# Seven-block products from output pair 4 in the four later feed-forward stages, their token sums made later and closer together

## The chip, the cores and the metric

One core of a Trainium2 chip runs the whole program. The metric is the device time of one execution in microseconds. The core has TensorE (matrix products into PSUM banks), VectorE, ScalarE and GpSimd, each with its own in-order stream of instructions, and SyncE, which issues most of the weight transfers. The engines meet only at semaphores.

## The reference, cut to what matters

512 tokens of width 1024 pass through two blocks of two layers each. The program holds six feed-forward products of one form (inner width 2816):

```python
def swiglu(h, w_in, w_out):
    g, u = jnp.split(h @ w_in, 2, axis=-1)
    return (jax.nn.silu(g) * u) @ w_out
```

The first four stand in a block with adaptive norms (a gain and a shift from a conditioning vector), the last two in one with plain RMS norms (`silu(g_part) * u_part`, the same product). Between them lie a pooling mixer, an attention, and two mixers of four branches. All is float32.

## The kernel before, in words

**Precision.** Each operand of a product is split into a high part (rounded to the fast float32 form, `F32R`) and a low part (the rest). A product of two is three matmuls: high by high, high by low, low by high. ScalarE makes high parts with a copy, VectorE low parts with a subtraction.

**Weights.** SyncE loads units of 128 columns by 1024 rows (512 KB) into four slots of `stage`. For each unit ScalarE makes `w_hi` (line 866, in `convert`), then VectorE `w_lo` (line 1600, its `convert`). Two pairs of `w_hi`/`w_lo` take turns, and a third pair (`third_hi`, `third_lo`) serves special units. A slot is loaded again once both parts of its unit are made.

**A feed-forward stage.** The 2816 inner columns are FC = 22 chunks of 128. An *output pair* is one chunk of gate and one of up, so there are 22 pairs, two to a *step* of four units: gate and up of the even pair, gate and up of the odd. In the text a *column* of a step is its c, 0 to 3. Plain form (`products`, lines 2604 to 2606): a unit is 8 chunks of the inner dimension times three matmuls of 512 tokens, 24 matmuls. ScalarE takes silu of the gate bank (`sg`), VectorE multiplies with the up bank, and the result is split for the output product, which follows the 22 pairs (`step_out`).

**The seven-block form.** In stages with `i >= SEVEN_FFN` (the third to the sixth) the later pairs are made otherwise. Gate and up columns, the two halves of the 1024 inner rows and the two halves of the tokens make a product of 2 by 2 by 2 blocks, done with seven block products instead of eight. A block (`block`, lines 2733 to 2735) is 4 chunks times three matmuls of 256 tokens, 12 matmuls. It needs sums of the weight blocks (`part_sums`, `second_sum`, `fourth_sum` on VectorE, then `sum_high` on ScalarE and `sum_low` on VectorE, anew for each pair) and four sums of the normed tokens, made once for a stage: `t_sum(0..3)` on VectorE, the high parts `t_high(0..3)` on ScalarE (line 955), the low parts `t_low(0..3)` on VectorE (line 1837). Sum 1 builds on sum 0, sum 3 on sum 1. In the third and fourth stages sums 1 to 3 are four operations each (line 1831), because a shift enters, in the fifth and sixth each is one (line 1825).

**Order in the opening.** `SEVEN_FROM` plain steps come first (`opening_step`), 3 before: pairs 0 to 5. In them VectorE and ScalarE have, beside their ordinary work, the token sums in an order written out by hand: `T_WORK` says after which (step, column) VectorE does which sum or low part, `T_HIGHS` after which ScalarE does which high part. In the last opening step, column 2, the weight sums of the first seven-block pair are made; `sum_high(0)` and `sum_low(0)` come ahead of `convert(c + 2)`, which prepares the row weights that the first block reads. Column 3 has the second weight sum, whose high part waits until TensorE has done all opening units. Then `seven_step` runs for the other steps, the first and last unrolled, the middle ones in a loop.

In the first block TensorE waits for `w_lo` of the row weights:

```python
pe.wait_ge(silu_ready, n.pair + 5)
pe.wait_ge(w_lo_ready, n.unit + 13)
block(GATE[0][:, 0:H], weights(n.unit + 12, 0), 1, of_h(4, 0), True).then_inc(product_done, 1)
```

**Late splits.** The products of seven-block pairs, and of the last opening step, are kept whole (`wk(k)`) and split late: `late_high(k)` on ScalarE (line 974) and `late_low(k)` on VectorE (line 1869), in the last pair and ahead of the output product. Products of earlier steps are split at once (lines 997 and 1905).

Of the kernel before, what the change touches and what calls it, by code (L numbers as in the profile page):

```python
# [37 lines left out]
WORDS = 8 * P  # L38
# [7 lines left out]
H = S // 2  # L46
SEVEN_FROM = 3
SEVEN_PAIRS = FC - 2 * SEVEN_FROM

# [49 lines left out]
def build(nc, A, out):  # L99
    ctx = ExitStack()  # L100
    with ctx:
# [95 lines left out]
        w_lo_ready = sem("w_lo_ready")  # L197
# [653 lines left out]
        def _(act):  # L851
# [80 lines left out]
            def ffn(i):  # L932
# [24 lines left out]
                def sum_high(which, at_, done):  # L957

                    dst = third_hi[:] if which == 0 else weights(n.unit + 13, 0)[0]
                    act.wait_ge(sums_ready, done)  # L960
                    nc.scalar.activation(dst, sums[:, which * 2 * S:(which + 1) * 2 * S], ACT.Copy) \
                        .then_inc(sum_hi_ready, 1)

                def late_high(k):

                    pb = 6 * SEVEN_PAIRS * (n.seven + 1)
                    act.wait_ge(prod_ready, n.pair + k + 1)
                    if k < 6:
                        act.wait_ge(unit_done, n.unit + 2 * FC - 2)
                    elif k < 18:  # L970
                        act.wait_ge(product_done, pb - (3 if k < 10 else 2 if k < 14 else 0))
                    else:
                        act.wait_ge(unit_done, n.unit + 2 * FC)
                    nc.scalar.activation(chunk(a_lo, k), wk(k), ACT.Copy).then_inc(a_hi_ready, 1)

                def opening_step(j):

                    for c in range(4):
                        p = n.pair + 2 * j + c // 2
                        raw = n.norm - 1 in RAW and j == 0  # L980
                        if j == 2 and c == 2:
                            sum_high(0, 0, 3 * SEVEN_PAIRS * n.seven + 3)
                        if j == 2 and c == 3:
                            act.wait_ge(unit_done, n.unit + 12)
                            sum_high(1, 0, 3 * SEVEN_PAIRS * n.seven + 2)
                        elif not raw or c == 3:
                            convert(c + 2, j)
                        if c % 2 == 0 and raw:
                            act.wait_ge(raw_scaled, RAW.index(n.norm - 1) // 2 * 2 + c // 2 + 1)
                            nc.scalar.activation(chunk(sg, p % 2), chunk(sg, p % 2), ACT.Silu).then_inc(silu_ready, 1)  # L990
                        elif c % 2 == 0:
                            act.wait_ge(unit_done, n.unit + 4 * j + c + 1)
                            act.wait_ge(prod_ready, p - 1)
                            nc.scalar.activation(chunk(sg, p % 2), GATE[p % 2][:], ACT.Silu).then_inc(silu_ready, 1)
                        elif j < 2:
                            act.wait_ge(prod_ready, p + 1)
                            nc.scalar.activation(chunk(a_lo, 2 * j + c // 2), chunk(prod, p % 2), ACT.Copy) \
                                .then_inc(a_hi_ready, 1)
                        if (j, c) in T_HIGHS:
                            t_high(T_HIGHS.index((j, c)))  # L1000

                def seven_step(step):
# [9 lines left out]
                    for r in range(2):  # L1012
# [6 lines left out]
                        if not first:  # L1019
# [9 lines left out]
                        act.wait_ge(w_loaded[slot], 16 * ((u0 + 2 * r + 2) // STAGES + 1) + 16 * step)  # L1029
                        nc.scalar.activation(weights(u0 + 12, 0)[0], stage[:, slot * WORDS:(slot + 1) * WORDS],  # L1030
                                             ACT.Copy).then_inc(w_hi_ready, 1)
# [4 lines left out]
                        if end:  # L1036
                            late_high(4)

                        act.wait_ge(product_done, count(6, 4))
                        nc.scalar.activation(snap_second, up[:, 0:H], ACT.Copy).then_inc(snap_ready, 1)  # L1040
                        if end:
                            for k in (5, 6, 7):
                                late_high(k)
                        else:
                            sum_high(1, r, count(3, 5))
# [16 lines left out]
                if i >= SEVEN_FFN:  # L1062
                    for j in range(SEVEN_FROM):
                        opening_step(j)
                    seven_steps(act, seven_step)
                    slot = (n.unit + 45) % STAGES
                    act.wait_ge(w_loaded[slot], 16 * ((n.unit + 45) // STAGES + 1))
                    nc.scalar.activation(weights(n.unit + 45, 0)[0], stage[:, slot * WORDS:(slot + 1) * WORDS],
                                         ACT.Copy).then_inc(w_hi_ready, 1)
                    fourth_snap(1, n.unit + 2 * FC, n.pair + FC - 1)  # L1070
                    for k in range(8, 16):
                        late_high(k)
                else:
                    looped(act, FC // 2, step_in)
# [508 lines left out]
        def _(dve):  # L1583
# [193 lines left out]
            def ffn(i, s):  # L1777
# [83 lines left out]
                def sum_low(which, done):  # L1861
                    hi, lo = (third_hi[:], third_lo[:]) if which == 0 else weights(n.unit + 13, 0)
                    dve.wait_ge(sum_hi_ready, done)
                    nc.vector.tensor_tensor(lo, sums[:, which * 2 * S:(which + 1) * 2 * S], hi.bitcast(F32),
                                            ALU.subtract).then_inc(sum_lo_ready, 1)
# [5 lines left out]
                def opening_step(j):  # L1871
                    f, u0 = n.seven, n.unit
                    for c in range(4):
                        p = n.pair + 2 * j + c // 2
                        u = u0 + 4 * j + c
                        raw = n.norm - 1 in RAW and j == 0
                        if j == 2 and c == 2:
                            dve.wait_ge(a_ready, n.pair + 4)
                            part_sums(u0 + 12, 0)
                            second_sum(u0 + 12, 0, 3 * SEVEN_PAIRS * f + 1)  # L1880
                            fourth_sum(u0 + 12, 0, 3 * SEVEN_PAIRS * f + 2)
                            sum_low(0, 2 * SEVEN_PAIRS * f + 1)
                        if j == 2 and c == 3:
                            t_low(3)
                            sum_low(1, 2 * SEVEN_PAIRS * f + 2)
                        elif not raw or c == 3:
                            convert(c + 2, j)
# [7 lines left out]
                        elif c % 2:  # L1895
                            dve.wait_ge(silu_ready, p + 1)
                            dve.wait_ge(unit_done, u + 1)
                            if j == 1:
                                dve.wait_ge(a_ready, p - 1)
                            dst = chunk(prod, p % 2) if j < 2 else wk(2 * j + c // 2)  # L1900
                            nc.vector.tensor_tensor(dst, chunk(sg, p % 2), UP[p % 2][:], ALU.mult).then_inc(prod_ready, 1)
                        if c % 2 and j < 2:
                            k = 2 * j + c // 2
# [15 lines left out]
                def seven_step(step):  # L1919
# [5 lines left out]
                    for r in range(2):  # L1925
# [12 lines left out]
                        if not end:  # L1938
                            second_sum(u, step, count(3, 4))
                            fourth_sum(u, step, count(3, 5))  # L1940
                        hi, lo = weights(u0 + 12, 0)
                        slot = u % STAGES
# [3 lines left out]
                        if end:  # L1946
                            late_low(4)

# [3 lines left out]
                        if end:  # L1952
                            for k in (5, 6, 7):
                                late_low(k)
# [6 lines left out]
                if i >= SEVEN_FFN:  # L1961
                    for j in range(SEVEN_FROM):
# [5 lines left out]
                    nc.vector.tensor_tensor(lo, stage[:, slot * WORDS:(slot + 1) * WORDS], hi.bitcast(F32),  # L1968
                                            ALU.subtract).then_inc(w_lo_ready, 1)
                    late_low(8)  # L1970
                    pairs = SEVEN_PAIRS * (n.seven + 1)
# [621 lines left out]
        def _(pe):  # L2593
# [92 lines left out]
            def ffn(i):  # L2686
# [64 lines left out]
                def seven_step(step):  # L2751
                    first, last = (isinstance(step, int) and step == s_ for s_ in (SEVEN_FROM, FC // 2 - 1))
                    f, u0, p0 = n.seven, n.unit, n.pair
                    rows = weights(u0 + 12, 0)
                    s21, s34 = weights(u0 + 13, 0), (third_hi, third_lo)

# [6 lines left out]
                    for r in range(2):  # L2763
# [24 lines left out]
                        if not (last and r == 1):  # L2788
                            if first and r == 0:
                                pe.wait_ge(silu_ready, p0 + 6)  # L2790
                            else:
# [9 lines left out]
                if i >= SEVEN_FFN:  # L2801
                    for j in range(SEVEN_FROM):
                        opening_step(j)
                    pe.wait_ge(silu_ready, n.pair + 5)
                    pe.wait_ge(w_lo_ready, n.unit + 13)
                    block(GATE[0][:, 0:H], weights(n.unit + 12, 0), 1, of_h(4, 0), True).then_inc(product_done, 1)
                    seven_steps(pe, seven_step)
# [713 lines left out]
for at_, step_ in enumerate(STAGE_ORDER):  # L3521
    if step_[0] in ("fox", "mix") or step_[0] == "ffn" and step_[1] >= 2:
# [5 lines left out]
KEPT = (3, 5, 7, 9)  # L3528
T_HIGHS = [(0, 3), (1, 1), (1, 3), (2, 0)]
T_WORK = {(0, 1): (("sum", 0),), (0, 3): (("sum", 1),), (1, 0): (("low", 0),), (1, 1): (("sum", 2),),  # L3530
          (1, 2): (("low", 1),), (1, 3): (("sum", 3),), (2, 0): (("low", 2),)}
TOTAL_UNITS = sum(UNITS_OF[s[0]] for s in STAGE_ORDER)
# [93 lines left out]
```

## Time and profile before

| | |
|---|---|
| median of 3 runs | 3654.19 us (3652.86 to 3658.12) |
| the profiled execution | 3653.87 us |
| its span, first to last instruction | 3652.1 us |
| TensorE busy | 3573.9 us (98%), 18986 matmuls |
| VectorE busy | 2157.6 us (59%) |
| ScalarE busy | 1604.8 us (44%) |
| mean granted TensorE clock | 0.993 |
| DMA | 388.72 MB, mean 106 GB/s |

The span is counted from the first instruction; 1.8 us of the execution lie around it. A granted clock of 1 is 2.4 GHz, 0.5 is 1.2 GHz. Durations of matmuls overlap with the next ones, so their rate is read from how many fit in a stretch and not from the duration of one. In the trace the four stages begin their seven-block products at 898.30, 1540.60, 2451.46 and 3362.25 us.

### The profile page before, as it was taken

The page shows a single profiled execution, that of the slowest core. Times are in us where ns is not written, and L with a number is a line of the kernel's source. Part 1 is how long each engine was busy: PE and PEld are TensorE (multiplying, and loading weights), DVE is VectorE, ACT ScalarE, POOL GpSimd, SP SyncE. Part 2 cuts the span into 40 slices and gives each one's busy share as a digit, 9 for nine tenths or more (in the row PEclk, how much of TensorE's full clock was granted, in tenths as well). Part 3 has the DMA queues.
Part 4 walks back from the last instruction along what each step waited for, and adds up shares of the span by engine and source line. Part 5 has one row for each costly group of instructions (what it writes and reads, how often), then busy time and mean ns, then how long its engine had stood idle before and what let it go on. Part 6 is the DMA issues. An engine that isn't in the chain of part 4 may idle for free.

```text
span 3652.1 us, 52186 instructions
## 1 busy us (share of the span) xinstructions
PE 3573.9 (98%) x18986; PEld 2922.6 (80%) x18986; DVE 2157.6 (59%) x3118; ACT 1604.8 (44%) x2666; POOL 87.2 (2%) x74
## 2 busy tenths in 40 slices
PE   7999999999999999999999999999999999999999
PEld 5888778888998777899867677889986767788997
DVE  6843488426873654687355556478735565647862
ACT  3232432224553554455354444355535454435552
POOL 0000100000000000000000000000000000000000
PEclk9999999999999999999999999999999999999999
DMA  9843278433333222333322222333332222233332
GB/s 313 275 127 95 85 251 278 140 99 91 104 104 94 58 58 58 93 104 100 95 80 65 62 70 61 91 93 104 101 103 72 69 58 74 57 91 93 104 104 87
DMA packets 643164, 388.72 MB, mean 106 GB/s; under 512 B 17969, under 2 KB 602545, under 8 KB 642993
## 3 DMA queue, kind: packets, MB, share of 16 engines
q1 hardware_dynamic: 640256, 381.41, 35.8%
q10 hardware_dynamic: 2736, 4.98, 0.4%
q8 instruction: 113, 1.85, 0.2%
q14 instruction: 59, 0.48, 0.0%
HBM read 384.23 MB, written 2.10 MB: 106 GB/s over the span
## 4 chain that ended last, share of the span: by engine, by line
PE 90%; DVE 5%; ACT 2%; issue 1%; SPq 1%; DMA 0%; POOL 0%; DVEq 0%; ACTq 0%; POOLq 0%
PE bank L2604 20%; PE bank L2605 20%; PE bank L2606 20%; PE bank L2733 6%; PE bank L2735 6%; PE bank L2734 6%; PE bank L2910 1%; PE bank L2975 1%; PE bank L2891 1%; PE bank L3126 1%; PE bank L2893 1%; PE bank L2892 1%; DVE w_lo L1600 1%; DVE work L2279 1%; PE bank L3192 1%
## 5 line engine op out<-in xcount | busy, mean ns | idle before, releaser
L1600 DVE TENSOR_TENSOR w_lo<-stage,w_hi 128x1024 fp32r<-128x1024 f32 x432 | 528.8, 1224 | 834.8 <-ACT w_hi L866 834.5
L2604 PE MATMUL bank<-h_hi,w_hi 128*128 128x512 f32 x2088 | 844.0, 404 | 13.3 <-ACT gs L1145 4.8
L2606 PE MATMUL bank<-h_hi,w_lo 128*128 128x512 f32 x2088 | 818.7, 392 | 0.0
L2605 PE MATMUL bank<-h_lo,w_hi 128*128 128x512 f32 x2088 | 818.6, 392 | 0.0
L866 ACT ACTIVATE w_hi<-stage 128x1024 fp32r<-128x1024 f32 x432 | 456.9, 1058 | 750.7 <-PE bank L2606 741.9
L2604 PEld LDWEIGHTS bank<-h_hi,w_hi 128*128 128x128 f32 x2088 | 395.1, 189 | 127.9 <-issue 30.0
L2605 PEld LDWEIGHTS bank<-h_lo,w_hi 128*128 128x128 f32 x2088 | 395.6, 189 | 84.1 <-issue 6.7
L2606 PEld LDWEIGHTS bank<-h_hi,w_lo 128*128 128x128 f32 x2088 | 395.0, 189 | 84.5
L2604 PE MATMUL bank<-a_lo,w_hi 128*128 128x512 f32 x704 | 274.6, 390 | 0.0
L2606 PE MATMUL bank<-a_lo,w_lo 128*128 128x512 f32 x704 | 274.0, 389 | 0.0
L2605 PE MATMUL bank<-a_hi,w_hi 128*128 128x512 f32 x704 | 274.0, 389 | 0.0
L2606 PEld LDWEIGHTS bank<-a_lo,w_lo 128*128 128x128 f32 x704 | 132.2, 188 | 27.7
L2605 PEld LDWEIGHTS bank<-a_hi,w_hi 128*128 128x128 f32 x704 | 132.2, 188 | 27.1
L2604 PEld LDWEIGHTS bank<-a_lo,w_hi 128*128 128x128 f32 x704 | 132.2, 188 | 26.9
L2735 PE MATMUL bank<-h_hi,w_lo 128*128 128x256 f32 x512 | 144.9, 283 | 0.0
L2733 PE MATMUL bank<-work_r,w_hi 128*128 128x256 f32 x512 | 144.9, 283 | 0.0
L2734 PE MATMUL bank<-work_r,w_hi 128*128 128x256 f32 x512 | 144.9, 283 | 0.0
L2735 PE MATMUL bank<-work_r,w_lo 128*128 128x256 f32 x512 | 144.9, 283 | 0.0
L2734 PE MATMUL bank<-h_lo,w_hi 128*128 128x256 f32 x512 | 144.9, 283 | 0.0
L2733 PE MATMUL bank<-h_hi,w_hi 128*128 128x256 f32 x512 | 144.9, 283 | 0.0
L2606 PE MATMUL bank<-a_hi,w_lo 128*128 128x512 f32 x352 | 136.9, 389 | 0.0
L2604 PE MATMUL bank<-a_hi,w_hi 128*128 128x512 f32 x352 | 136.9, 389 | 0.0
(421 smaller groups left out, 6734.9 us busy)
## 6 DMA issues: line engine op xcount, KB each, us to landing
stage<-in_ffn_w_in SPq DMA_DIRECT2D x176, 512.0 KB, 3.9
stage<-in_w_in SPq DMA_DIRECT2D x108, 512.0 KB, 3.8
stage<-in_w_gate_up SPq DMA_DIRECT2D x88, 512.0 KB, 3.8
ada_stage<-in_ada_w SPq DMA_DIRECT2D x128, 256.0 KB, 4.4
work<-in_ada_w SPq DMA_DIRECT2D x128, 256.0 KB, 6.5
stage<-in_ffn_w_out SPq DMA_DIRECT2D x64, 512.0 KB, 3.9
stage<-in_w_down SPq DMA_DIRECT2D x32, 512.0 KB, 4.2
stage<-in_ffn_w_out SPq DMA_DIRECT2D x32, 384.0 KB, 3.4
```

Of the source, the lines that this page charges most:

```text
L866: nc.scalar.activation(weights(u, per * i)[0], stage[:, slot * WORDS:(slot + 1) * WORDS], ACT.Copy).then_inc(w_hi_ready, 1)
L1600: nc.vector.tensor_tensor(lo, stage[:, slot * WORDS:(slot + 1) * WORDS], hi.bitcast(F32), ALU.subtract).then_inc(w_lo_ready, 1)
L2279: nc.vector.tensor_tensor(part, part, other, ALU.mult).then_inc(hfac_ready, 1)
L2604: nc.tensor.matmul(dst, wh, chunk(hi, k), start=first and a == 0, stop=False)
L2605: nc.tensor.matmul(dst, wh, chunk(lo, k), start=False, stop=False)
L2606: ins = nc.tensor.matmul(dst, wl, chunk(hi, k), start=False, stop=last and a == len(ks) - 1)
L2733: nc.tensor.matmul(dst, wh, xh, start=first and k == 0, stop=False, skip_group_check=True)
L2734: nc.tensor.matmul(dst, wh, xl, start=False, stop=False, skip_group_check=True)
L2735: ins = nc.tensor.matmul(dst, wl, xh, start=False, stop=k == 3, skip_group_check=True)
L2891: nc.tensor.matmul(bank[7][:], wh, hi, start=c == 0, stop=False)
L2892: nc.tensor.matmul(bank[7][:], wh, lo, start=False, stop=False)
L2893: ins = nc.tensor.matmul(bank[7][:], wl, hi, start=False, stop=c == 1)
```

## The change

`SEVEN_FROM` goes from 3 to 2. Pairs 4 and 5 of the third to the sixth stage are made in seven blocks too (18 pairs instead of 16 in each), and two opening steps are left. What was tied to the last opening step moves to step 1: the weight sums, `sum_high` and `sum_low`, and the uses of `weights(...)` with a number in them are written by `SEVEN_FROM`. The products of pairs 2 and 3 are now split late. `late_high` and `late_low` of chunks 2 and 3 take the place in the last pair that chunk 4 had, chunks 4 to 6 that of 5 to 7, and chunk 7 joins the later ones. `T_WORK` and `T_HIGHS` are rewritten: the sums begin one column later in step 0 and end in step 1, column 1; the high parts 0 and 1 come together in step 0, column 3; low part 3 comes after the product of step 1, column 3, where it was ahead of it and of the second weight sum's low part.

```diff
-SEVEN_FROM = 3
+SEVEN_FROM = 2
 ...
-                    dst = third_hi[:] if which == 0 else weights(n.unit + 13, 0)[0]
+                    dst = third_hi[:] if which == 0 else weights(n.unit + 4 * SEVEN_FROM + 1, 0)[0]
 ...
-                    if k < 6:
+                    if k < 4:
+                        pass
+                    elif k < 6:
                         act.wait_ge(unit_done, n.unit + 2 * FC - 2)
 ...
-                        if j == 2 and c == 2:
+                        if j == SEVEN_FROM - 1 and c == 2:
                             sum_high(0, 0, 3 * SEVEN_PAIRS * n.seven + 3)
-                        if j == 2 and c == 3:
-                            act.wait_ge(unit_done, n.unit + 12)
+                        if j == SEVEN_FROM - 1 and c == 3:
+                            act.wait_ge(unit_done, n.unit + 4 * SEVEN_FROM)
                             sum_high(1, 0, 3 * SEVEN_PAIRS * n.seven + 2)
 ...
-                        elif j < 2:
+                        elif j < SEVEN_FROM - 1:
 ...
-                        if (j, c) in T_HIGHS:
-                            t_high(T_HIGHS.index((j, c)))
+                        for which in T_HIGHS.get((j, c), ()):
+                            t_high(which)
 ...
                         if end:
-                            late_high(4)
+                            for k in (2, 3):
+                                late_high(k)
 ...
-                            for k in (5, 6, 7):
+                            for k in (4, 5, 6):
                                 late_high(k)
 ...
-                    for k in range(8, 16):
+                    for k in range(7, 16):
                         late_high(k)
 ...
-                        if j == 2 and c == 2:
-                            dve.wait_ge(a_ready, n.pair + 4)
-                            part_sums(u0 + 12, 0)
-                            second_sum(u0 + 12, 0, 3 * SEVEN_PAIRS * f + 1)
-                            fourth_sum(u0 + 12, 0, 3 * SEVEN_PAIRS * f + 2)
+                        if j == SEVEN_FROM - 1 and c == 2:
+                            dve.wait_ge(a_ready, n.pair + 2 * SEVEN_FROM - 2)
+                            part_sums(u0 + 4 * SEVEN_FROM, 0)
+                            second_sum(u0 + 4 * SEVEN_FROM, 0, 3 * SEVEN_PAIRS * f + 1)
+                            fourth_sum(u0 + 4 * SEVEN_FROM, 0, 3 * SEVEN_PAIRS * f + 2)
                             sum_low(0, 2 * SEVEN_PAIRS * f + 1)
-                        if j == 2 and c == 3:
-                            t_low(3)
+                        if j == SEVEN_FROM - 1 and c == 3:
                             sum_low(1, 2 * SEVEN_PAIRS * f + 2)
 ...
+                    late_low(7)
                     late_low(8)
 ...
-                    pe.wait_ge(silu_ready, n.pair + 5)
-                    pe.wait_ge(w_lo_ready, n.unit + 13)
-                    block(GATE[0][:, 0:H], weights(n.unit + 12, 0), 1, of_h(4, 0), True).then_inc(product_done, 1)
+                    pe.wait_ge(silu_ready, n.pair + 2 * SEVEN_FROM - 1)
+                    pe.wait_ge(w_lo_ready, n.unit + 4 * SEVEN_FROM + 1)
+                    block(GATE[0][:, 0:H], weights(n.unit + 4 * SEVEN_FROM, 0), 1, of_h(4, 0), True).then_inc(product_done, 1)
 ...
-T_HIGHS = [(0, 3), (1, 1), (1, 3), (2, 0)]
-T_WORK = {(0, 1): (("sum", 0),), (0, 3): (("sum", 1),), (1, 0): (("low", 0),), (1, 1): (("sum", 2),),
-          (1, 2): (("low", 1),), (1, 3): (("sum", 3),), (2, 0): (("low", 2),)}
+T_HIGHS = {(0, 3): (0, 1), (1, 0): (2,), (1, 1): (3,)}
+T_WORK = {(0, 2): (("sum", 0),), (0, 3): (("sum", 1),), (1, 0): (("low", 0), ("sum", 2)),
+          (1, 1): (("sum", 3), ("low", 1)), (1, 2): (("low", 2),), (1, 3): (("low", 3),)}
```

## Rows read from the trace of the kernel before

**Rows 1.** The page: busy time (share) xinstructions, and the chain by engine.
```profile
PE 3573.9 (98%) x18986; PEld 2922.6 (80%) x18986; DVE 2157.6 (59%) x3118; ACT 1604.8 (44%) x2666; POOL 87.2 (2%) x74
...
PE 90%; DVE 5%; ACT 2%; issue 1%; SPq 1%; DMA 0%; POOL 0%; DVEq 0%; ACTq 0%; POOLq 0%
```

**Rows 2.** Waits of TensorE, 838 to 1062 us: total, times, longest.
```profile
PE bank L2733 <- ACT rstd L1049: 0.5, 1, 0.5
```

**Rows 3.** Windows by engine (us, busy (x), clock, DMA); timeline of TensorE.
```profile
843.90:898.30 54.40, 54.40 (x242) 45.05 (x240) 32.32 (x42) 20.31 (x25) 0.00 (x0) 1.00 0.34 98
898.30:1058.14 159.84, 159.84 (x1333) 159.78 (x1331) 131.54 (x173) 92.81 (x160) 0.00 (x0) 1.00 0.37 107
...
2451.46 0.28 PE L2733 MATMUL bank<-h_hi,w_hi 128*128 128x256 f32 x1
```

**Rows 4.** Timeline of VectorE, third stage: start, us, line, out<-in [idle before].
```profile
859.26 1.67 DVE L1831 SCALAR_TENSOR_TENSOR work<-work,mod 128x256 f32<-128x256 f32 x4
...
870.14 0.16 DVE L1828 TENSOR_TENSOR shift_step<-mod 128x4 f32<-128x4 f32 x1
870.34 1.68 DVE L1831 SCALAR_TENSOR_TENSOR work<-work,shift_step 128x256 f32<-128x256 f32 x4
...
889.91 0.68 DVE L1901 TENSOR_TENSOR work<-sg,bank 128x512 f32<-128x512 f32 x1
890.51 0.69 DVE L1848 TENSOR_TENSOR sums<-stage 128x512 f32<-128x512 f32 x1
...
894.38 1.23 DVE L1864 TENSOR_TENSOR third_lo<-sums,third_hi 128x1024 fp32r<-128x1024 f32 x1 [1.13 <-ACT third_hi L961]
895.52 1.22 DVE L1600 TENSOR_TENSOR w_lo<-stage,w_hi 128x1024 fp32r<-128x1024 f32 x1
...
901.33 0.69 DVE L1848 TENSOR_TENSOR sums<-stage 128x512 f32<-128x512 f32 x1
...
904.47 1.22 DVE L1944 TENSOR_TENSOR w_lo<-stage,w_hi 128x1024 fp32r<-128x1024 f32 x1
```

**Rows 5.** Timeline of ScalarE, third stage.
```profile
858.52 1.05 ACT L955 ACTIVATE work_r<-work 128x1024 fp32r<-128x1024 f32 x1
860.48 1.06 ACT L866 ACTIVATE w_hi<-stage 128x1024 fp32r<-128x1024 f32 x1 [0.91 <-PE bank L2606]
...
893.28 1.06 ACT L961 ACTIVATE third_hi<-sums 128x1024 fp32r<-128x1024 f32 x1 [4.54 <-DVE sums L1858]
894.25 1.04 ACT L866 ACTIVATE w_hi<-stage 128x1024 fp32r<-128x1024 f32 x1
...
898.50 1.06 ACT L961 ACTIVATE w_hi<-sums 128x1024 fp32r<-128x1024 f32 x1 [2.72 <-PE bank L2606]
```

**Rows 6.** Timeline of VectorE, fifth stage.
```profile
2414.56 1.22 DVE L1825 TENSOR_TENSOR work<-work 128x1024 f32<-128x1024 f32 x1
```

**Rows 7.** Timeline of ScalarE, fifth stage.
```profile
2414.77 1.04 ACT L866 ACTIVATE w_hi<-stage 128x1024 fp32r<-128x1024 f32 x1
```

**Rows 8.** Timeline of ScalarE at the end of the third stage's seven-block pairs.
```profile
1060.77 4.27 ACT L974 ACTIVATE a_lo<-work 128x512 fp32r<-128x512 f32 x8
1066.02 1.06 ACT L866 ACTIVATE w_hi<-stage 128x1024 fp32r<-128x1024 f32 x1 [0.98 <-PE bank L2606]
```

**Rows 9.** Windows, TensorE alone: us, busy (x), granted clock, DMA share, GB/s.
```profile
412.42:414.56 2.14, 0.00 (x2) 1.00 0.54 214
414.72:418.13 3.41, 3.41 (x17) 0.50 0.00 0
...
448.86:455.69 6.83, 5.86 (x11) 0.50 0.00 0
468.35:470.22 1.87, 0.00 (x1) 1.00 0.89 302
470.22:475.00 4.78, 4.78 (x21) 1.00 0.64 189
...
1206.62:1210.03 3.41, 3.41 (x9) 0.50 0.52 144
```

More of the change, by code:

```diff
@@ L1029, in seven_step @@
                         act.wait_ge(w_loaded[slot], 16 * ((u0 + 2 * r + 2) // STAGES + 1) + 16 * step)
-                        nc.scalar.activation(weights(u0 + 12, 0)[0], stage[:, slot * WORDS:(slot + 1) * WORDS],
+                        nc.scalar.activation(weights(u0 + 4 * SEVEN_FROM, 0)[0], stage[:, slot * WORDS:(slot + 1) * WORDS],
                                              ACT.Copy).then_inc(w_hi_ready, 1)
@@ L1861, in sum_low @@
                 def sum_low(which, done):
-                    hi, lo = (third_hi[:], third_lo[:]) if which == 0 else weights(n.unit + 13, 0)
+                    hi, lo = (third_hi[:], third_lo[:]) if which == 0 else weights(n.unit + 4 * SEVEN_FROM + 1, 0)
                     dve.wait_ge(sum_hi_ready, done)
@@ L1897, in opening_step @@
                             dve.wait_ge(unit_done, u + 1)
-                            if j == 1:
+                            if 0 < j < SEVEN_FROM - 1:
                                 dve.wait_ge(a_ready, p - 1)
-                            dst = chunk(prod, p % 2) if j < 2 else wk(2 * j + c // 2)
+                            dst = chunk(prod, p % 2) if j < SEVEN_FROM - 1 else wk(2 * j + c // 2)
                             nc.vector.tensor_tensor(dst, chunk(sg, p % 2), UP[p % 2][:], ALU.mult).then_inc(prod_ready, 1)
-                        if c % 2 and j < 2:
+                        if c % 2 and j < SEVEN_FROM - 1:
                             k = 2 * j + c // 2
@@ L1940, in seven_step @@
                             fourth_sum(u, step, count(3, 5))
-                        hi, lo = weights(u0 + 12, 0)
+                        hi, lo = weights(u0 + 4 * SEVEN_FROM, 0)
                         slot = u % STAGES
@@ L1946, in seven_step @@
                         if end:
-                            late_low(4)
+                            for k in (2, 3):
+                                late_low(k)
                         dve.wait_ge(product_done, count(6, 5))
@@ L1952, in seven_step @@
                         if end:
-                            for k in (5, 6, 7):
+                            for k in (4, 5, 6):
                                 late_low(k)
@@ L2753, in seven_step @@
                     f, u0, p0 = n.seven, n.unit, n.pair
-                    rows = weights(u0 + 12, 0)
-                    s21, s34 = weights(u0 + 13, 0), (third_hi, third_lo)
+                    rows = weights(u0 + 4 * SEVEN_FROM, 0)
+                    s21, s34 = weights(u0 + 4 * SEVEN_FROM + 1, 0), (third_hi, third_lo)
                     def count(per, plus):
@@ L2789, in seven_step @@
                             if first and r == 0:
-                                pe.wait_ge(silu_ready, p0 + 6)
+                                pe.wait_ge(silu_ready, p0 + 2 * SEVEN_FROM)
                             else:
```

## The prediction

> **What bounds the kernel now.** I read the page first: TensorE is busy 98% of the span and holds 90% of the chain that ended last [rows 1]. The span is TensorE's time, so an edit pays only by taking TensorE cycles away and costs only by letting it wait. Next, the waits of the third feed-forward stage from its first product to its last: in 220 us TensorE waits once, 0.5 us [rows 2]. The same view of the fifth stage says the same.
>
> Then the cost of a product. One output pair (128 gate and 128 up columns) takes 48 matmuls of 512 columns in the plain form, 84 of 256 columns in the seven-block form. The durations (390 and 280 ns) overlap, so I take the rate from the windows. The plain stretch 843.90 to 898.30 holds 240 matmuls (242 shown, two begun before it): 54.40/240 = 226.7 ns. The seven-block stretch 898.30 to 1058.14 holds 111 blocks of 12: 159.84/1332 = 120.0 ns [rows 3]. So a pair costs 48 x 0.2267 = 10.88 us plain, 84 x 0.120 = 10.08 us in seven blocks, and a unit (24 plain matmuls) 5.44 us.
>
> **What the change takes away.** Two more pairs (4 and 5) of each of four stages: 8 x 0.80 = 6.4 us less. The 0.5 us wait of the last pair stays. That is 0.18% of the run. About 0.2% (7.3 us) is what a measurement of this kernel can tell from no change.
>
> The Trainium skill (TensorE: Matmul & The Clock Gate, section "Back-to-back issue gap") gives about columns/2.4 + 2.5 ns, which is 216 and 109 ns here; by that the estimate for a pair is 10.36 against 9.17 us, and for the eight pairs 9.5 us. The measured 120 ns of the 256-column form decides against it.
>
> **What the change moves.** Before, three opening steps (12 units, 65 us) covered the preparation of four token sums: four sums and four low parts on VectorE, four high parts on ScalarE. Now all but the last low part has to happen ahead of block products that begin after two steps. The work itself is not larger, but it is a chain across two in-order engines. I follow it in the third stage with the durations and hand-over times of the rows: an operation of 1024 columns starts its successor on VectorE after 1.14 us, on ScalarE after 0.97; the other engine sees its end 0.03 us later. The seven-block part was to begin at 898.30 and would now be due at 898.30 - 4 x 5.44 = 876.54.
>
> - Step 0, column 3: sum 1 (four operations, L1831) runs 859.26 to 860.93 [rows 4]. ScalarE, after high part 0 (858.52, [rows 5]), now waits for it: high part 1 at 860.96. The conversion w_hi of unit 6, queued behind it, moves from 860.48 to 861.93, end 862.98. TensorE needs unit 6 at 865.66: hidden.
> - Step 1, column 0 on VectorE: w_lo of unit 6 863.01, low 0 864.15, sum 2 865.29; from its small operation to its end 1.88 us (870.14 to 872.02, [rows 4]), so 867.17. ScalarE: high part 2 at 867.20, and behind it w_hi of unit 7 at 868.17, end 869.22.
> - Column 1: w_lo of unit 7 869.25 to 870.48; TensorE needs it at 871.10: 0.6 us spare. Product 870.39, sum 3 871.00 to 872.67, low 1 872.61; the next can start at 873.75.
> - Column 2: the four weight sums take from 890.51 until 893.28, when ScalarE takes up `third_hi` [rows 4, 5], 2.77 us; so `third_hi` at 876.52, and w_hi of unit 8 behind it at 877.49, end 878.53. VectorE: `third_lo` 877.61, w_lo of unit 8 878.75 to 879.97.
>
> Unit 8 is the row weights of the first block product. Before, its w_lo was made from 895.52 to 896.74, 1.56 us ahead of need [rows 4]. Now TensorE, due at 876.54, waits until 880.00: a stall of **3.46 us**. The fourth stage runs the same operations with the same shapes, so I give it the same stall.
>
> In the fifth and sixth stages the sums are single operations of 1.22 us, but they start later against the products: sum 1 ends at 2415.78, 3.0 us before unit 6 is due (4.7 us in the third stage) [rows 6]. High part 1 2415.81; w_hi of unit 6 2416.78 instead of 2414.77 [rows 7]; its w_lo ends at 2419.08, and unit 6 is due at 2418.82 (the first block, 2451.46 [rows 3], less six units): 0.3 us of waiting. Low 0 2419.00, sum 2 2420.14, high 2 2421.39, w_hi of unit 7 2422.36, its w_lo ends 2424.67 against 2424.56: 0.14 more. Product 2424.58, sum 3 2425.19, low 1 2426.33, weight sums 2427.47, `third_hi` 2430.24, w_hi of unit 8 2431.21, `third_lo` 2431.33, w_lo of unit 8 ends 2433.70. The block product, due at 2429.70 + 0.44, waits 3.58 us. Together **4.02 us**.
>
> What is late next? Low 2 and the second weight sum follow on VectorE and end at 882.23; the third block needs it at 880.00 + 2.88 = 882.88. ScalarE's high part of it (once tied to the end of the last plain unit, 898.50, [rows 5]) now comes before the first block. Low 3, moved behind the product, delays the next weight sums by 1.1 us: they start 3.87 us after the first block instead of 3.03 (901.33, [rows 4]), and the row weights of the next pair end 8.2 us after it. Before it was 7.4 (904.47 + 1.22), and the sixth block needs them at 8.64: no stall, 0.4 us spare. Were that gone, each 0.1 us late would cost 0.1 us a stage.
>
> **The tail.** Chunks 2 and 3 of the products are now converted late: two more ScalarE operations of 0.53 us and two VectorE operations of 0.6. One of each goes into idle time of the last pair, one falls behind the last pair, where eight late operations take 4.27 us on ScalarE and ScalarE is then idle 0.98 us before the next w_hi [rows 8]. That idle covers 0.53; I cost it at nothing, and at 4 x 0.5 = 2 us if the cover is gone. They replace operations inside the opening, which are no longer on the path. Weight loads keep their trigger (w_lo) and the stage buffer is four units deep; unit 9, which the weight sums need, is asked for once w_lo of unit 5 is made, which is before sum 1 (859.26), over 14 us ahead of 873.75: nothing.
>
> Stalls: 2 x 3.46 + 2 x 4.02 = 15.0. Less 6.4 gained: **+8.6 us**.
>
> **TensorE's clock.** Each stall leaves the array idle some 3.3 us. After the 2.14 us of idle before 414.56 the granted clock fell to 0.50 for 3.41 us (1.2 instead of 2.4 GHz); after 1.87 us it stayed at 1.00 [rows 9]. Five idle stretches are longer than 2.1 us, that one the shortest, and half rate followed all five. In such a stretch, from 1206.62, 9 matmuls of 512 columns were under way, one of them begun before; at full rate it would be 15. At half rate a 256-column matmul takes an estimated 213 ns (half of what 512 columns take there, 3.41/8), so 3.41 us holds 16 instead of 28: 1.5 us lost, less where the slow stretch begins in the idle time. I take 1.15 per stall, 4.6 in all; the bounds are 0 and 4 x 3.0 (two such stretches each, as at 448.86, 6.83 us [rows 9]).
>
> Sum: 8.6 + 4.6 = 13.2. The profiled execution has 3653.87 us (span 3652.1 and 1.8 around it), the median of the three is 3654.19. So 3653.87 + 13.2 = 3667.1, and on the median **3667.4 us**, +0.36%.
>
> **Rivals.**
> 1. Stalls, no slow clock: 3654.2 + 8.6 = 3662.8, +0.24%. For it: 1.87 us of idle did nothing. Against it: five of five longer ones did.
> 2. The stall is half as long: what ScalarE's waits for the sums put ahead of the conversions (w_hi of unit 6 alone is 1.45 us late, 861.93 against 860.48) passes beside other work. 15.0/2 - 6.4 = +1.1, and the clock perhaps +1: 3655 to 3657, the same.
> 3. The other side: w_lo of unit 8 is ready when due. VectorE is busy 32.3 of the 54.4 us before the first block [rows 3], so throughput is there; this decides if the chain of column 2 begins 3.5 us earlier than 873.75. Then only the 6.4 us remain: 3647.8, -0.18%, the same by the bound. Against it: sum 3 sits behind the product of column 1, and what follows adds up to 6.2 us from fixed durations.
> 4. A 256-column matmul in steady state costs half of a 512-column one, 113.3 ns, and nothing stalls: 84 x 0.1133 = 9.52 us, 1.36 us a pair, 8 x 1.36 = 10.9: 3643.3, faster by 0.30%. The windows measure 120.0 ns over 1332 matmuls, so next to no chance. The Trainium skill, in the section named above, puts it at 109 ns.
> 5. More is late: the 0.4 us of spare at the sixth block goes, and two slow stretches follow each stall. 3667.4 + 4 x 1.85 + 4 x 0.5 = 3677.
>
> **Numbers.** Forecast 0.48, rival 1 0.25, rival 2 0.11, rival 3 0.06, rival 4 0.01, rival 5 0.09. Slower (above 3661.5): 0.48 + 0.25 + 0.09, less 0.04 for a rival 1 that ends just under the bound, 0.78. Same: 0.11 + 0.06 + 0.04 = 0.21. Faster: 0.01. The range 3657 to 3673 leaves out rivals 3, 4 and 5 and the lower part of rival 2, some 0.2. The forecast's own range is 3663 to 3672.
>
> **What would show it.** In the changed kernel: one TensorE wait of about 3.5 us in each of stages 3 to 6, at the first 256-column product, put down to VectorE's w_lo (the conversion at L1600 here); two small ones before units 6 and 7 in stages 5 and 6 alone; granted clock 0.50 for 3.4 us behind most of them; in each stage 168 more matmuls of 256 columns and 96 fewer of 512; no new wait in the tail. Wrong would be: no wait at the first block (chain shorter than its rows say), waits at the third or sixth block, or a seven-block pair that does not take 10.08 us.

## The result and the profile after

| | before | after |
|---|---|---|
| median of 5 runs | 3654.43 us (3652.86 to 3658.12) | 3671.84 us (3667.81 to 3673.62) |
| ratio, 95% interval | | 1.0043 (1.0032 to 1.0053) |
| the profiled execution's span | 3652.1 us | 3670.6 us |
| matmuls | 18986 | 19274 |

The medians differ by 17.4 us, 0.48%: the change makes the kernel slower. The ratio is estimated at 1.0043, and its interval is 12 to 19 us. The forecast was +13.2 us (3667.4), with a range from 3657 to 3673; the median lies 4.4 us above the forecast and 1.2 us inside the end of the range.

The page of the changed kernel, busy time (share) xinstructions, then the chain that ended last by engine; these answer to [rows 1]:

```profile
PE 3578.9 (98%) x19274; PEld 2938.8 (80%) x19274; DVE 2197.6 (60%) x3182; ACT 1628.7 (44%) x2722; POOL 87.1 (2%) x74
...
PE 86%; DVE 7%; ACT 3%; issue 2%; SPq 1%; DMA 0%; POOL 0%; DVEq 0%; ACTq 0%; POOLq 0%
```

TensorE's share of the chain fell from 90 to 86%, VectorE's rose from 5 to 7%: the end now hangs on VectorE at some places. TensorE's waits over the whole span say where (total, times, longest), and its waits in the third stage, 838 to 1068 us, answer to [rows 2]:

```profile
PE bank L2737 <- DVE w_lo L1603: 13.3, 4, 3.3
...
PE bank L2737 <- DVE w_lo L1603: 3.3, 1, 3.3
PE bank L2737 <- ACT rstd L1052: 0.5, 1, 0.5
...
PE bank L2608 <- DVE w_lo L1603: 0.3, 1, 0.3
```

The last line is of the fifth stage, the wait before unit 6. Line 2737 is the block product's first matmul, line 1603 the `w_lo` conversion: four waits, one a stage. None of these was there before. In the timeline of TensorE the wait is the idle time ahead of the first 256-column matmul:

```profile
878.91 0.39 PE L2610 MATMUL bank<-h_hi,w_lo 128*128 128x512 f32 x1
882.64 0.55 PE L2737 MATMUL bank<-h_hi,w_hi 128*128 128x256 f32 x1 [3.35 <-DVE w_lo L1603]
882.99 0.41 PE L2738 MATMUL bank<-h_lo,w_hi 128*128 128x256 f32 x1
```

And this is the chain behind it, VectorE in the third stage (start, duration); these answer to [rows 4]. This execution reached the stage 2.6 us later than that of the kernel before, so 2.6 us come off for a comparison:

```profile
861.86 1.67 DVE L1834 SCALAR_TENSOR_TENSOR work<-work,mod 128x256 f32<-128x256 f32 x4
865.60 1.22 DVE L1603 TENSOR_TENSOR w_lo<-stage,w_hi 128x1024 fp32r<-128x1024 f32 x1 [2.08 <-ACT w_hi L866]
...
871.81 1.23 DVE L1603 TENSOR_TENSOR w_lo<-stage,w_hi 128x1024 fp32r<-128x1024 f32 x1 [2.08 <-ACT w_hi L866]
...
873.55 1.67 DVE L1834 SCALAR_TENSOR_TENSOR work<-work,mod 128x256 f32<-128x256 f32 x4
875.14 1.22 DVE L1840 TENSOR_TENSOR work_r<-work,work_r 128x1024 fp32r<-128x1024 f32 x1
876.27 0.69 DVE L1851 TENSOR_TENSOR sums<-stage 128x512 f32<-128x512 f32 x1
...
880.14 1.23 DVE L1867 TENSOR_TENSOR third_lo<-sums,third_hi 128x1024 fp32r<-128x1024 f32 x1 [1.12 <-ACT third_hi L961]
881.28 1.22 DVE L1603 TENSOR_TENSOR w_lo<-stage,w_hi 128x1024 fp32r<-128x1024 f32 x1
```

ScalarE beside it, which answers to [rows 5]:

```profile
861.12 1.05 ACT L955 ACTIVATE work_r<-work 128x1024 fp32r<-128x1024 f32 x1
863.55 1.06 ACT L955 ACTIVATE work_r<-work 128x1024 fp32r<-128x1024 f32 x1 [1.39 <-DVE work L1834]
864.52 1.04 ACT L866 ACTIVATE w_hi<-stage 128x1024 fp32r<-128x1024 f32 x1
...
869.77 1.06 ACT L955 ACTIVATE work_r<-work 128x1024 fp32r<-128x1024 f32 x1 [3.73 <-DVE work L1834]
870.74 1.04 ACT L866 ACTIVATE w_hi<-stage 128x1024 fp32r<-128x1024 f32 x1
```

The two engines take turns at waiting. ScalarE idles 1.39 us for sum 1 and 3.73 us for sum 2 with a weight conversion queued behind, VectorE then idles 2.08 us each time for that conversion. VectorE ends `w_lo` of unit 8 at 881.28 + 1.22 = 882.50, and the block starts 0.14 us later.

**Where the time went.** I take the length of a stage from the last `bank<-sq,consts` product of its norm (line 2655 before, 2659 after) to that of the next norm, or to the end of the span for the sixth stage; the four of before are 353.4, 355.6, 348.9 and 352.8 us. "Slow" is the time at a granted clock of 0.50 in the stage. The stretch at 0.50 that every span ends with begins behind the last matmul (before: at 3650.57, the last matmul ends at 3648.91), so it costs TensorE nothing and is not counted.

| us against before | third | fourth | fifth | sixth | four stages | all else | span |
|---|---|---|---|---|---|---|---|
| after | +3.26 | +4.55 | +2.58 | +4.06 | +14.5 | +4.1 | +18.6 |
| slow in it | 3.4 | 6.8 | 0 | 3.4 | | 54.6 (before 47.8) | |

The four stages hold 14.5 of the 18.6 us. The rest is code that the diff doesn't touch. It does not stay the same between executions: in those below it goes from -3.3 us, with 34.1 us at half rate in this part, to +8.2 us, with 64.9.

### The profile page after: what moved, and what is told of

It is laid out like the page before. It is cut to its first block, busy times and chain, and to the rows that moved or that the text cites. A ratio compares the mean times of both kernels' runs of the same rounds, so it can differ in the third digit from the quotient of the medians.

```text
span 3670.6 us, 53192 instructions
## 1 busy us (share of the span) xinstructions
PE 3578.9 (98%) x19274; PEld 2938.8 (80%) x19274; DVE 2197.6 (60%) x3182; ACT 1628.7 (44%) x2722; POOL 87.1 (2%) x74
## 4 chain that ended last, share of the span: by engine, by line
PE 86%; DVE 7%; ACT 3%; issue 2%; SPq 1%; DMA 0%; POOL 0%; DVEq 0%; ACTq 0%; POOLq 0%
PE bank L2608 18%; PE bank L2610 18%; PE bank L2609 18%; PE bank L2737 7%; PE bank L2738 7%; PE bank L2739 7%; DVE w_lo L1603 1%; PE bank L2914 1%; PE bank L2979 1%; PE bank L2895 1%; DVE work L2283 1%; ACT w_hi L866 1%; PE bank L2897 1%; PE bank L2896 1%; PE bank L3130 1%
## 5 line engine op out<-in xcount | busy, mean ns | idle before, releaser
L2608 PE MATMUL bank<-h_hi,w_hi 128*128 128x512 f32 x1960 | 793.8, 405 | 14.2 <-ACT gs L1148 4.8
L2610 PE MATMUL bank<-h_hi,w_lo 128*128 128x512 f32 x1960 | 769.0, 392 | 0.0
L2609 PE MATMUL bank<-h_lo,w_hi 128*128 128x512 f32 x1960 | 768.2, 392 | 0.0
L2608 PEld LDWEIGHTS bank<-h_hi,w_hi 128*128 128x128 f32 x1960 | 370.9, 189 | 124.0 <-issue 31.9
L2609 PEld LDWEIGHTS bank<-h_lo,w_hi 128*128 128x128 f32 x1960 | 371.3, 189 | 79.4 <-issue 6.7
L2610 PEld LDWEIGHTS bank<-h_hi,w_lo 128*128 128x128 f32 x1960 | 370.6, 189 | 79.4
L2737 PE MATMUL bank<-h_hi,w_hi 128*128 128x256 f32 x576 | 165.7, 288 | 13.3 <-DVE w_lo L1603 13.3
L2738 PE MATMUL bank<-h_lo,w_hi 128*128 128x256 f32 x576 | 165.3, 287 | 0.0
L2739 PE MATMUL bank<-h_hi,w_lo 128*128 128x256 f32 x576 | 165.2, 287 | 0.0
L2737 PE MATMUL bank<-work_r,w_hi 128*128 128x256 f32 x576 | 163.3, 283 | 0.0
L2738 PE MATMUL bank<-work_r,w_hi 128*128 128x256 f32 x576 | 163.2, 283 | 0.0
```

What stands on the lines that cost most here:

```text
L2608: nc.tensor.matmul(dst, wh, chunk(hi, k), start=first and a == 0, stop=False)
L2609: nc.tensor.matmul(dst, wh, chunk(lo, k), start=False, stop=False)
L2610: ins = nc.tensor.matmul(dst, wl, chunk(hi, k), start=False, stop=last and a == len(ks) - 1)
L2737: nc.tensor.matmul(dst, wh, xh, start=first and k == 0, stop=False, skip_group_check=True)
L2738: nc.tensor.matmul(dst, wh, xl, start=False, stop=False, skip_group_check=True)
L2739: ins = nc.tensor.matmul(dst, wl, xh, start=False, stop=k == 3, skip_group_check=True)
```

## The experiments

Each kernel was timed in five rounds against the kernel before.

**The changed kernel again.**

> The changed kernel once more, beside the others on one chip. If the stalls make the loss, four TensorE waits of 3.3 us again at the first 256-column product of the four stages, and a time 13 to 18 us above the kernel before. Where the granted clock falls behind them may differ from the first execution.

Median 3672.41, ratio 1.0049 (1.0035 to 1.0063). The four waits are there again, 3.3 us each. Its stages are +4.42, +4.41, +4.05, +2.57 us, together +15.5, with slow time of 6.8, 6.8, 3.4 and 0 us. The rest of its span is 3.3 us shorter than before, with 34.1 us of slow time. So the stages repeat within what the clock does, and the +4.1 us of the first execution's rest does not. The profiled execution (3665.98) is the fastest of its five.

**Hand-over: high part 1 behind the conversion.**

```diff
-T_HIGHS = {(0, 3): (0, 1), (1, 0): (2,), (1, 1): (3,)}
+T_HIGHS = {(0, 3): (0,), (1, 0): (1, 2), (1, 1): (3,)}
```

> The high part of token sum 1 is moved on ScalarE from step 0, column 3 to step 1, column 0, behind the conversion of unit 6; VectorE's order is untouched. Theory, a chain of hand-overs between ScalarE and VectorE: w_hi of units 6 and 7 is no longer held up, the first block waits 2.0 us instead of 3.5 in all four stages and the small waits before units 6 and 7 in the fifth and sixth stages go, so 3654.4 - 6.4 + 8.0 = 3656.0, up to 3658 if the clock falls once or twice. Rival, VectorE has too much work in the two steps: its work is the same, so the stalls stay and the time is 3668 to 3672.

Median 3663.46, ratio 1.0024 (1.0013 to 1.0035). Waits of TensorE over the third stage, then over the fifth (to 2620 us):

```profile
PE bank L2737 <- DVE w_lo L1603: 1.9, 1, 1.9
PE bank L2737 <- ACT rstd L1052: 0.5, 1, 0.5
```

Both stages have the same two lines: the first block waits 1.9 us instead of 3.3, and the wait before unit 6 is gone. No work was taken from VectorE, only the place of one ScalarE copy. So the stall is a chain of hand-overs, not a want of VectorE time. The time is above my 3656 to 3658. The stages are +2.03, +0.58, +2.05, +2.07: the fourth, where the clock stayed up, is near my figure, and the three others had 3.4 us of slow time each after an idle stretch of only 1.93 us. The rest had 2.9 us more.

**Row weights ahead of the weight sum's parts.**

```diff
                         if j == SEVEN_FROM - 1 and c == 2:
+                            convert(c + 2, j)
                             sum_high(0, 0, 3 * SEVEN_PAIRS * n.seven + 3)
...
                             fourth_sum(u0 + 4 * SEVEN_FROM, 0, 3 * SEVEN_PAIRS * f + 2)
+                            convert(c + 2, j)
                             sum_low(0, 2 * SEVEN_PAIRS * f + 1)
...
-                        elif not raw or c == 3:
+                        elif (not raw or c == 3) and (j, c) != (SEVEN_FROM - 1, 2):
                             convert(c + 2, j)
```

The last of these is in both engines' `opening_step`.

> In step 1, column 2 the conversion of the row weights (unit 8) is put ahead of the first weight sum's high part on ScalarE and ahead of its low part on VectorE, still behind the four weight sums. Theory: the first block waits 1.1 us (third and fourth stages) and 1.3 us (fifth and sixth), and the wait comes again in part at the third block, 0.5 us, for the second weight sum, and 0.2 at the sixth; with the 0.4 us before units 6 and 7 in the fifth and sixth stages 8.9 us of stalls: 3654.4 - 6.4 + 8.9 = 3656.9. Rival, the whole chain binds and not the place of this conversion: the third block waits some 3 us instead, and the time is 3665 or more.

Median 3658.59, ratio 1.0008 (0.9999 to 1.0017). Waits of TensorE over the third stage (in this kernel line 2739 is the block's first matmul, 1604 `w_lo`, 1868 the low part of a weight sum):

```profile
PE bank L2739 <- DVE w_lo L1604: 1.0, 1, 1.0
PE bank L2739 <- ACT rstd L1053: 0.5, 1, 0.5
PE bank L2739 <- DVE w_lo L1868: 0.4, 1, 0.4
```

The wait at the first block shrinks to 1.0 us and comes back with 0.4 at the third, as expected; the 0.2 us at the sixth did not show. The stages are +0.48, +0.48, +1.07, +1.08 with no slow time at all, together +3.1 (expected 8.9 - 6.4 = +2.5). Idle stretches of 1.0 us did not bring the clock down in any of the four stages.

**The stall filled with work, six matmuls.**

```diff
                     pe.wait_ge(silu_ready, n.pair + 2 * SEVEN_FROM - 1)
+                    busy_work(bank[7], 6)
                     pe.wait_ge(w_lo_ready, n.unit + 4 * SEVEN_FROM + 1)
```

> Six float32 matmuls of 512 columns into an unused bank are put ahead of the wait for the row weights of the first block, about 2.8 us of work for TensorE inside the stall (their results are used by nothing). The wait itself stays, so the engine is as late as in the changed kernel, but not idle. Theory, slow clock behind the stall is part of the loss: granted clock 1.00 in the 7 us behind the first block of all four stages, and 4.6 to 6 us less than the changed kernel, about 3654.4 + 8.6 = 3663.0. Rival, the clock is no part of it: the same time as the changed kernel, 3668 to 3672.

Median 3671.87, ratio 1.0043 (1.0030 to 1.0057): no gain, and by the time alone the rival would stand. The timeline of TensorE shows that the test was spoilt:

```profile
878.51 5.31 PE L2648 MATMUL bank<-consts 128*128 128x512 f32 x12
883.26 0.69 PE L2737 MATMUL bank<-h_hi,w_hi 128*128 128x256 f32 x1
```

The six float32 matmuls (each of them two records) held TensorE for 883.26 - 878.51 = 4.75 us at the least, not 2.8, and so held the first block back themselves: `w_lo` had been ready since 881.86. Their records begin every 0.43 us, the twelfth at 883.23, and the second matmul of the block begins only at 883.78, so the six are worth 12 x 0.43 = 5.1 us. There was no slow time in the four stages (+3.54, +3.57, +4.16, +4.19).

**The same with four.**

```diff
-                    busy_work(bank[7], 6)
+                    busy_work(bank[7], 4)
```

> As the run with six matmuls in the stall, but four of them, since six took 4.75 us (from 878.51 to 883.26 in its trace) and pushed the first block 1.3 us past the end of the wait. Four should take 3.2 us, just less than the wait of 3.46. Theory, the slow clock behind the stalls is part of the loss: clock 1.00 behind all four first blocks, the third and fourth stages 1.9 to 2.1 us longer than before, the fifth and sixth 2.4 to 2.7, together 8.6 to 9.6 where the changed kernel had 14.5 and 15.5 in two executions, and a median near 3654.5 + 9 = 3663.5. Rival, the loss behind the stalls has another cause than the clock: the stages stay at 3.3 us and more each, and the median at 3668 or more.

Median 3665.55, ratio 1.0029 (1.0017 to 1.0042). The granted clock of the first 3.4 us of the blocks, third and fourth stage, windows of TensorE alone (us, busy (x), clock, DMA): after the change

```profile
882.64:886.05 3.41, 3.41 (x17) 0.56 0.51 154
1528.30:1531.71 3.41, 3.41 (x16) 0.50 0.52 154
2443.75:2447.16 3.41, 3.41 (x28) 1.00 0.52 154
```

(the third line is the fifth stage) and with the filled stall, from the first blocks of the same two stages on

```profile
879.35:882.76 3.41, 3.41 (x29) 1.00 0.51 154
1522.05:1525.46 3.41, 3.41 (x29) 1.00 0.53 154
```

At 0.50 there are 16 matmuls in 3.41 us where the fifth stage, at 1.00, has 28; with the stall filled there are 28 in each, and one record of the filling work that still runs. The four filling matmuls begin at 875.94 in the third stage; their eight records at 0.43 us make 3.4 us, not 3.2, and just fill the wait: `w_lo` is ready at 879.29, and the block starts at 879.35. With the filled stall there is no slow time in any of the four stages. They are +1.95, +1.91, +2.50, +2.50 us, together +8.9; the median lies 2 us above my 3663.5, the stages are inside what I expected of them. Since the wait for `w_lo` is the same, the difference to the changed kernel is the clock: 14.5 - 8.9 = 5.6 us in one execution, 15.5 - 8.9 = 6.6 in the other. The changed kernel has the same control in itself: its two stages in which the clock stayed up, the fifth of the first execution and the sixth of the second, are +2.58 and +2.57 us, beside +2.50 for both with the stall filled.

**The order alone, with three opening steps.** `SEVEN_FROM = 3` and the late splits of before, with the new `T_WORK` and `T_HIGHS`.

> Three opening steps as before (seven blocks from pair 6), with the new order of the token sums and of their high and low parts alone, and the late splits as before. Theory: the order itself holds up the conversions, so TensorE waits about 0.8 us before unit 8 in the third and fourth stages and 1.4 us before units 6 to 8 together in the fifth and sixth, and nothing at the first block: 3654.4 + 4.3 = 3658.7. Rival, the order costs nothing where there are three steps: 3654.4.

Median 3664.22, ratio 1.0021 (1.0012 to 1.0030). The theory's waits, in the third stage and in the fifth (line 2607 is the first matmul of a plain unit here):

```profile
PE bank L2607 <- DVE w_lo L1603: 0.8, 1, 0.8
...
PE bank L2607 <- DVE w_lo L1603: 1.0, 2, 0.7
```

The stages are +1.03, +1.04, +1.60, +1.64, together +5.3 (expected 4.3). So the order costs by itself, even where there is a step more to hide it; it does not explain all of the 9.4 us of the median. In the profiled execution the rest is 8.2 us longer, with 64.9 us of slow time there instead of 47.8. I leave open whether that is more than luck; the interval (4 to 11 us) holds both.

**No token sums.** Their work is left out, and the blocks read the normed tokens instead.

```diff
+T_HIGHS = {}
+T_WORK = {}
...
-                        if first and r == 0:
-                            pe.wait_ge(t_lo_ready, 4 * f + which + 1)
+                        pass
...
-                        return t_part(which, 0)[:, k * H:(k + 1) * H], t_part(which, 1)[:, k * H:(k + 1) * H]
+                        return of_h(0, 0)(k)
```

> The changed kernel without token sums: their work on VectorE and ScalarE is left out, TensorE does not wait for them and reads the normed tokens in their place, with the same number and shape of matmuls. Theory, the token sums in two steps make the stall: no wait at the first block, and only the gain of the eight pairs is left, 3654.4 - 6.4 = 3648.0. Rival, the weight sums or the weights themselves come too late after two steps: a wait of 1 us or more stays at the first or third block, 3652 or more.

Median 3650.45, ratio 0.9987 (0.9978 to 0.9996). No wait at a first or third block; TensorE's waits over the third stage are one line, the 0.5 us of before:

```profile
PE bank L2737 <- ACT rstd L1052: 0.5, 1, 0.5
```

The stages are -1.62, -1.60, -1.57, -1.61, together -6.4: the gain of the eight pairs, to the tenth of a microsecond.

**All the work in another order.**

```diff
+T_HIGHS = {(0, 2): (0, 1), (0, 3): (2,), (1, 0): (3,)}
+T_WORK = {(0, 1): (("sum", 0),), (0, 2): (("sum", 1), ("sum", 2)), (0, 3): (("sum", 3),),
+          (1, 0): (("low", 0), ("low", 1), ("low", 2)), (1, 2): (("low", 3),)}
+RAW_HIGHS = {(0, 3): (0,), (1, 0): (1, 2), (1, 3): (3,)}
+RAW_WORK = {(0, 1): (("sum", 0),), (0, 3): (("sum", 1),), (1, 0): (("low", 0), ("sum", 2), ("low", 1)),
+            (1, 2): (("sum", 3), ("low", 2)), (1, 3): (("low", 3),)}
```

The second pair of tables is used where `n.norm - 1 in RAW` (the fifth and sixth stages).

> All work of the changed kernel in another order. Third and fourth stages: token sum 0 in step 0, column 1, sums 1 and 2 in column 2, sum 3 in column 3, high parts 0 and 1 in column 2, 2 in column 3, 3 in step 1, column 0; low parts 0 to 2 in step 1, column 0, low part 3 in column 2. Fifth and sixth: sum 2 with low 0 and 1 in step 1, column 0, sum 3 and low 2 behind the weight sums in column 2, high part 3 and low part 3 in column 3. Theory: no wait at the first block in any stage, some 0.5 us at the third and sixth block in the fifth and sixth stages: 3654.4 - 6.4 + 1.0 = 3649.0. Rival, the work does not fit into two steps in any order: stalls of 1.5 us or more in each stage, 3654 or more.

Median 3649.96, ratio 0.9991 (0.9982 to 1.0000). TensorE's waits over the fifth stage; the third has the first line alone:

```profile
PE bank L2737 <- ACT rstd L1052: 0.5, 1, 0.5
PE bank L2737 <- DVE w_lo L1867: 0.2, 1, 0.2
```

VectorE in the third stage, for comparison with the chain above:

```profile
852.04 1.67 DVE L1834 SCALAR_TENSOR_TENSOR work<-work,mod 128x256 f32<-128x256 f32 x4
853.62 0.16 DVE L1831 TENSOR_TENSOR shift_step<-mod 128x4 f32<-128x4 f32 x1
853.81 1.67 DVE L1834 SCALAR_TENSOR_TENSOR work<-work,shift_step 128x256 f32<-128x256 f32 x4
...
868.96 0.69 DVE L1851 TENSOR_TENSOR sums<-stage 128x512 f32<-128x512 f32 x1
...
873.97 1.22 DVE L1603 TENSOR_TENSOR w_lo<-stage,w_hi 128x1024 fp32r<-128x1024 f32 x1
```

Sums 1 and 2 now fill a gap in step 0, the weight sums begin at 868.96 and `w_lo` of unit 8 is ready at 875.19, 1.55 us ahead of the first block at 876.74. The stages are -1.61, -1.61, -0.93, -0.93, together -5.1.

**Again, beside the filled stall.**

> The kernel with the new order once more, beside the filled stall on one chip. Its stages should again be 1.6 us shorter than before in the third and fourth and 0.9 in the fifth and sixth, 5.0 together: 3654.5 - 5.0 = 3649.5. Rival, the first result was luck of the clock in parts that no edit touches: the median within 1 us of the kernel before.

Median 3654.22 against 3654.36, ratio 0.9997 (0.9988 to 1.0006). The stages repeat, -1.59, -1.56, -0.95, -0.94, together -5.0. The whole does not: the eleven runs go from 3648.2 to 3658.3 us. So the new order beats the changed kernel by some 18 to 22 us (by the medians, which were taken at different times, each beside the kernel before) and is 5 us shorter than before in the stages it touches; whether the program is faster than before by more than it scatters is not settled by 22 runs.

## Why the prediction was right

- **The gain.** 8 x 0.80 = 6.4 us: shown, -6.4 in the stages without token sums. The rate for half the columns would have given 10.9, and the rule of the Trainium skill (TensorE: Matmul & The Clock Gate, section "Back-to-back issue gap"), which it gives for the isolated gap of a matmul, 9.5 as an estimate; the 120 ns of [rows 3] decided rightly, as the -6.4 us show.
- **The stall.** The worked chain put `w_lo` of unit 8 at 878.75 in the third stage; it started at 881.28 - 2.60 = 878.68. The first block was worked out to start at 880.00 and did at 882.64 - 2.60 = 880.04. All four waits are of 3.3 us, and the small one before unit 6 of the fifth stage, worked out as 0.3, is there with 0.3 (0.2 in the sixth stage). The one before unit 7, worked out as 0.14, is too small for the view of waits; in the timeline unit 7 starts at 2434.74, 0.13 us behind 2429.17 + 5.44. The cause is shown from two sides: the stall goes when the token sums go, and it shrinks by 1.4 us when one ScalarE copy changes its place. The two other orders (rows first, the new order) shorten it as their chains say. Together the stages cost 8.9 us with the clock held up, against 8.6 worked out; the 0.3 is under 0.1 us a wait above the sum of hand-overs.
- **What is late next, and the tail.** No wait at the third or sixth block after the first, none new in the tail: only the 0.5 us of before. That the covered late splits cost nothing holds, as the run without token sums has them too and gives all 6.4 us.
- **The clock.** The mechanism held, the size was low. Slow time followed three of four stalls in each of two executions. 3.4 us of it cost 1.3 to 1.6 us (third stage 3.26 - 1.95, sixth 4.06 - 2.50), 6.8 us cost 2.5 to 2.6 (4.55 - 1.91). Per stall that is 5.6/4 = 1.4 and 6.6/4 = 1.65 us where I took 1.15. This is the term of the sum that was mis-sized: 5.6 to 6.6 us, not 4.6. The estimated 213 ns of a 256-column matmul at half rate was right: behind the stall they begin every 0.21 us. What was low is the 1.15: it took 0.35 us off the 1.5 of a slow stretch of 3.4 us, which cost 1.3 to 1.6, and counted on one such stretch a stall, where three of the eight stalls had 6.8 us. The step behind it, that half rate comes after 2.1 us of idle and not below, was too sharp: it came after 1.93 us three times in four, and in the second execution of the changed kernel 2.21 us of idle before 1209.88 passed without it. The trace of before, read only for stretches above 2.1 us, already had one below it (windows of TensorE alone):

```profile
2975.57:2977.61 2.04, 0.00 (x0) 1.00 0.22 64
2978.14:2981.55 3.41, 3.41 (x9) 0.50 0.00 0
```

- **The rest of the difference.** 8.9 + 5.6 to 6.6 is 14.5 to 15.5 us. The medians say 17.4 and 17.9, with intervals from 12 us up. So of the 4.4 us between the forecast and the median, 1 to 2 us are the clock's term, 0.3 the stalls, and 2 to 3 us have no place in the sum. They are not located. The time of the code that no edit touches moves with the clock's slow stretches there (rest -3.3 us with 34 us slow, +4.1 with 55, +8.2 with 65), but chance alone is not shown, and one thing speaks against it: in all ten comparisons, those without a stall too, the difference of the medians lies above that of the four stages, by 0.2 us (new order, first time) to 4.9 us (its second time), 2.4 us in the mean. (The stages are those of one profiled execution each.) What causes it stays open.
- **The rivals.** Without slow clock (3662.8): the filled stall is this case, +8.9 us in its stages, but the changed kernel is not. Half the stall and no stall: excluded by the four waits. A 256-column matmul at 113.3 ns: excluded by the -6.4 us. More is late: no wait came at the sixth block, but the two slow stretches (6.8 us) that rival 5 put behind each stall came behind one of four stalls in the first execution and behind two of four in the second. Yet rival 3 named the right quantity, a chain of column 2 that begins 3.5 us earlier; in the new order it does (868.96 - 0.20 against 873.75, by 5 us), and the stall is gone.

## What to carry to other kernels

When a stage is shortened, the work that its length covered has to be followed as a chain through the in-order queues, not as busy shares: VectorE was busy 60% and TensorE still waited, because each ScalarE copy that waits for a fresh sum holds the weight conversion queued behind it. Put what waits for a new result behind what is ready, and use the idle gaps that lie further ahead. A wait of TensorE can cost more than its length through the clock: here the 13.3 us of waits cost another 5.6 to 6.6 us, and waits of 1.0 us nothing. Whether several short waits are cheaper than one long one was not tried.

## What the runs showed of the hardware that I had not expected

- Float32 matmuls of 512 columns took 0.86 us each, 3.8 times the 226.7 ns of one matmul of the split form. The profile shows each as two records of 0.59 us that overlap; the twelve of six matmuls begin at 878.51 to 883.23, every 0.43 us, so the rate is read from their starts and not from their durations.
- Whether the clock falls after an idle stretch of about 2 us differs from execution to execution. After 2.21 us at one place that no edit touches (it ends at 1206.35 in the kernel before, at 1212.24 in the changed one) it fell in five of the eleven profiled executions and stayed up in six. After the 3.3 us of the stalls it fell six times of eight, after 1.93 us three times of four, after 1.0 us never in four.
- Executions of one kernel spread over 10 us (3648.2 to 3658.3 in eleven runs), more than the 6.4 us that were to be gained. In the profiled ones the shortest and the longest time of untouched code go with its least and its most time at half rate (34 and 65 us); between them, at 47.8 us in five executions, it still differs by 3.0 us.
